# Weight-block sums of a gated-mixer decoder layer: added into SBUF during the MLP, or made in DRAM beforehand

## The chip, the core and the metric

The kernel is one program on one core of a Trainium2 chip. The metric is device time in microseconds of one execution, median of the runs shown. The core has five engines with a queue each: TensorE (PE; its weight loads are PEld), VectorE (DVE), ScalarE (ACT), GpSimd (POOL) and SyncE (SP), which here only issues transfers. All transfers, whoever issues them, run on the core's 16 DMA engines. Transfers that add to what stands at their destination are issued by POOL (queue q0); plain ones are issued by SP (q1) or ACT (q10).

## The reference

One layer, 512 tokens of width 1024, all float32:

```python
h = rms_norm(x, norm_mix_pre)
z = h @ w_in                                  # 10 parts of 1024 columns
y_a = a_b * causal_dwconv(a_c * a_h, conv_a_w)                   # 3 taps
y_c = silu(layer_norm(causal_dwconv(c_a * sigmoid(c_g), conf_dw_w) + conf_dw_b))   # 31 taps
y_s = spatial_gating(gelu(s_u), gelu(s_v), ...)                  # causal 128 x 128 per head
merged = sigmoid(g_a)*(y_a @ w_branch[0]) + sigmoid(g_c)*(y_c @ w_branch[1]) + sigmoid(g_s)*(y_s @ w_branch[2])
x = x + rms_norm(merged @ w_out, norm_mix_post)
f = square(relu(rms_norm(x, norm_ffn_pre) @ w_ff1)) @ w_ff2      # 1024 -> 4096 -> 1024
x = x + rms_norm(f, norm_ffn_post)
```

## The kernel before

**Units.** Weights are loaded and used in units of 512 KB, [128 partitions x 1024] float32, numbered 0 to 223. Each unit is split in two for precision: ACT copies it to `w_hi` (float32r, line 683), DVE subtracts to get `w_lo` (line 1066), and TensorE makes three products, hi*hi, lo*hi and hi*lo (lines 1590 to 1594, or 1775 to 1779 in the MLP's up product). `w_hi` and `w_lo` are rings of four units (`RING`), so ACT and DVE split unit u+4 when TensorE has done unit u. Up to the MLP the raw weights go through two slots (`RAW`): SP loads unit u (line 457) when DVE has split unit u-2.

**Stages**, by the profile's time: units 0 to 7, the spatial branch's `v` (to 52 us); the mixer, eight tiles of six units with the taps of both convolutions on DVE (52 to 322 us); the gates, 24 pairs of a gate unit and a branch unit (322 to 585 us), in whose first eight pairs DVE has the last nine taps of each convolution tile; the output projection (to 629 us); the MLP (629 to 953 us).

**Beside the gates**, POOL sums the convolution's channels tile by tile (`chan_sum`, lines 625 and 628), each when DVE has finished the tile's taps, and TensorE needs the sum behind the tenth pair (line 1736). In a pair ACT first makes a tanh of the gate (line 825), then splits unit u+4, then waits for the branch unit and splits unit u+5; DVE splits, does taps, gates the branch with the tanh (line 1249), splits, does taps.

**The MLP** runs in four quarters (`q`) of the hidden width, each an UP and a DOWN product. Both are 2 x 2 block products done in seven multiplications instead of eight: products 1, 2, 3 take one block of the weights, product 5 the sum of two blocks, 7 of two, 6 of three, 4 of four (by adding one more block to what product 5, then 6, left in its slot). A block is two units. The sums are made in SBUF: POOL issues transfers of a block's unit that add to a slot (`add_block`, line 646, 50 of 512 KB), and for product 7 SP loads a second block into slots 0 and 1 beside it (`side_load`) and DVE adds them (`sum_beside`, line 1389, 14 times). SP's order (`ff_load`, line 506) is written out by hand with waits behind sums. At the product changes TensorE waits until DVE has joined earlier products out of PSUM (line 1399).

**The start.** While TensorE does units 0 to 7, the row factors 1/rms are found; ACT copies them to `row_rstd` (line 758) behind the split of unit 6, and TensorE's unit 4 waits for it before its last block. DVE multiplies a table of taps by 0.5 (`cols`) right behind its first splits.

Of the kernel before, what the change touches and what calls it, by code (L numbers as in the profile page):

```python
# [25 lines left out]
F32 = mybir.dt.float32  # L26
F32R = mybir.dt.float32r
ALU = mybir.AluOpType
# [60 lines left out]
LOADED = {1: (0, 0), 2: (1, 0), 3: (1, 1), 5: (0, 0)}  # L89
ADDED = {5: (0, 1), 6: (1, 1), 4: (1, 0), 7: (0, 1)}  # L90
SLOTS = 10


def slot_of(f, product):
    return {1: 0, 2: 2, 3: 6, 7: 6}.get(product, 8 if f == DOWN else 4)
# [12 lines left out]
def stands_alone(u):  # L108

    return piece_of(u)[:3] == (QUARTERS - 1, DOWN, 7)  # L110


def is_loaded(u):
    return piece_of(u)[2] in LOADED or stands_alone(u)


def by_dma(u):
    return piece_of(u)[2] in (5, 6, 4) or stands_alone(u)


def ff_slot(u):
    _, f, product, h = piece_of(u)
    return (4 if stands_alone(u) else slot_of(f, product)) + h


def earlier_in_slot(u):
    return [v for v in range(U_FF, u) if ff_slot(v) == ff_slot(u)]


def ff_loads(u):  # L130
    many = sum(is_loaded(v) for v in earlier_in_slot(u))
    return 16 * (U_FF // RAW + 2 * many + 1 if ff_slot(u) < RAW else many + 1)


def side_loads(q, f):

    return 16 * (U_FF // RAW + 2 * (2 * q + f) + 2)


def sums_beside(q, f, h):  # L140

    return 2 * (2 * q + f) + h + 1


def sums_in_slot(u):
    return 16 * (sum(by_dma(v) for v in earlier_in_slot(u)) + 1)


def source(u, added=False):

    q, f, product, h = piece_of(u)
    k_half, n_half = (ADDED if added else LOADED)[3 if not added and stands_alone(u) else product]
    if f == DOWN:
        k_half = 1 - k_half
    at = 2 * (2 * k_half + n_half) if f == UP else CH * n_half + 2 * k_half
    return U_FF + (2 * q + f) * BLOCK_UNITS + at + h
# [81 lines left out]
def build(nc, x_d, xt_d, gain_d, units_d, cols_d, rows_d, ws_d, bs_d, out_d):  # L238
    kept_d = nc.dram_tensor("mixed_kept", (SEQ, D), F32, kind="Internal").ap()
    with ExitStack() as ctx:  # L240
# [108 lines left out]
        summed = sem("summed")  # L349
        raw_added = [sem(f"raw_added{n}") for n in range(SLOTS)]  # L350
# [104 lines left out]
        def _(sp):  # L455
# [29 lines left out]
            def ff_load(q, f, product, halves=(0, 1)):  # L485
                for h in halves:
                    u = ff_unit(q, f, product, h)
                    slot = ff_slot(u)
                    if earlier_in_slot(u) and slot < RAW:
                        sp.wait_ge(summed, sums_beside(q, f, h) - 2)  # L490
                    elif earlier_in_slot(u):
                        sp.wait_ge(w_lo_ready, earlier_in_slot(u)[-1] + 1)
                    elif slot < 2:
                        sp.wait_ge(w_lo_ready, u - RAW + 1)
                    elif slot < 4:
                        sp.wait_ge(spatial_done, KT)
                        sp.wait_ge(a_step, 3 * KT)
                        sp.wait_ge(s_step, 3 * KT)
                    elif slot < 6:
                        sp.wait_ge(y_c_lo, KT)  # L500
                    elif slot < 8:
                        sp.wait_ge(mixed_in, 4 * CH)
                    else:
                        sp.wait_ge(mixed_kept[CH - 2 + h], 16)
                        sp.wait_ge(sumsq_ready, 4 * CH)
                    sp.dma_start(slots[slot], units_d[source(u)]).then_inc(raw_loaded[slot], 16)
# [10 lines left out]
            for c in range(CH):  # L517
                if c == CH - 1:
                    ff_load(0, UP, 3)
# [1374 lines left out]
```

## Time and profile before

| | us |
|---|---|
| median of 3 runs | 960.39 |
| lowest, highest | 959.5, 963.52 |
| the profiled execution | 961.98 |
| its span, first to last instruction | 960.2 |
| TensorE busy | 949.0 |
| DVE, ACT, POOL busy | 730.8, 431.0, 104.5 |
| DMA moved | 142.84 MB |

The span is what the trace covers; the profiled execution took 1.8 us more around it. A busy time is what an engine's instructions cover, ends of matmuls modelled. A view of waits counts idle time of an engine ahead of an instruction and names what ended it; the chain that ended last is followed back from the last instruction, each step to what released it.

### The profile page before, as it was taken

Reading aid. Unit: us, or ns where it says so; the run is one execution under the profiler, and the core shown is the slowest. Engines: PE = TensorE matmul, PEld = TensorE weight load, DVE = VectorE, ACT = ScalarE, POOL = GpSimd, SP = SyncE. Lnnn points to the kernel's source line nnn. Section 1 sums busy time; section 2 is a strip of 40 time slices with the busy share of each in tenths; the row PEclk is TensorE's granted clock in tenths of the full one; section 3 lists DMA queues with packets and bytes.
Section 4 is the critical chain, followed back from the end, with each engine's and each line's share of the span. In section 5 each row is a group of like instructions: output and inputs, shape, how many; then the busy total and the mean of one; then the engine's idle time right before and its main releaser. Section 6 shows DMA issues by size and latency. Waiting matters only on the chain.

```text
span 960.2 us, 13424 instructions
## 1 busy us (share of the span) xinstructions
PE 949.0 (99%) x4838; PEld 808.8 (84%) x4838; DVE 730.8 (76%) x854; ACT 431.0 (45%) x534; POOL 104.5 (11%) x128
## 2 busy tenths in 40 slices
PE   9999999999999999999999999999999999999997
PEld 7788888888888888888888888899889889979985
DVE  4579888888888988886585344599975886796698
ACT  6543333333333322224374223467645745754674
POOL 1100001000100011113100000131101101111111
PEclk9999999999999999999999999999999999999999
DMA  8333333323223232224235333477989579778974
GB/s 313 106 113 105 110 93 93 110 93 93 93 93 103 66 103 94 88 88 131 88 101 207 113 106 112 173 203 198 255 267 244 158 211 244 169 180 256 257 189 131
DMA packets 40731, 142.84 MB, mean 149 GB/s; under 512 B 4720, under 2 KB 4848, under 8 KB 40688
## 3 DMA queue, kind: packets, MB, share of 16 engines
q1 hardware_dynamic: 31728, 111.32, 33.4%
q0 software_dynamic: 7712, 27.27, 15.5%
q10 hardware_dynamic: 1248, 3.67, 1.0%
q8 instruction: 27, 0.44, 0.2%
q14 instruction: 16, 0.13, 0.0%
HBM read 138.05 MB, written 4.19 MB: 148 GB/s over the span
## 4 chain that ended last, share of the span: by engine, by line
PE 82%; DMA 10%; DVE 4%; ACT 2%; issue 1%; SPq 0%; POOL 0%; ACTq 0%; DVEq 0%
PE ps L1590 25%; PE ps L1594 25%; PE ps L1592 25%; DMA glu<-units_in 6%; DMA raw_d<-units_in 2%; PE ps L1775 2%; DVE w_lo L1066 2%; PE ps L1777 2%; PE ps L1779 2%; ACT w_hi L683 1%; DMA raw<-units_in 1%; PE ps L1716 1%; DMA cols<-cols_in 1%; DMA glu<-xt_in 1%; ACT h L960 0%
## 5 line engine op out<-in xcount | busy, mean ns | idle before, releaser
L1590 PE MATMUL ps<-a_hi,w_hi 128*128 128x512 f32 x576 | 225.7, 392 | 0.0
L1592 PE MATMUL ps<-a_lo,w_hi 128*128 128x512 f32 x576 | 224.2, 389 | 0.0
L1594 PE MATMUL ps<-a_hi,w_lo 128*128 128x512 f32 x576 | 224.1, 389 | 0.0
L1066 DVE TENSOR_TENSOR w_lo<-raw,w_hi 128x1024 fp32r<-128x1024 f32 (+1 forms) x125 | 153.1, 1228 | 87.8 <-ACT w_hi L683 87.2
L683 ACT ACTIVATE w_hi<-raw 128x1024 fp32r<-128x1024 f32 (+1 forms) x125 | 130.2, 1048 | 184.7 <-PE ps L1594 103.7
L1149 DVE SCALAR_TENSOR_TENSOR conf<-glu,cols,conf (+1 forms) x240 | 186.8, 778 | 27.5 <-DVE conf L1149 26.4
L1590 PEld LDWEIGHTS ps<-a_hi,w_hi 128*128 128x128 f32 x576 | 108.1, 188 | 22.7 <-issue 0.5
L1592 PEld LDWEIGHTS ps<-a_lo,w_hi 128*128 128x128 f32 x576 | 108.2, 188 | 22.6 <-issue 0.5
L1594 PEld LDWEIGHTS ps<-a_hi,w_lo 128*128 128x128 f32 x576 | 108.2, 188 | 22.5
L1066 DVE TENSOR_TENSOR w_lo<-glu,w_hi 128x1024 fp32r<-128x1024 f32 x56 | 67.6, 1221 | 38.1 <-ACT w_hi L683 37.9
L1590 PE MATMUL ps<-w_hi,h_hi 128*128 128x512 f32 x224 | 88.0, 393 | 0.6 <-DVE wide L1424 0.2
L1594 PE MATMUL ps<-w_hi,h_lo 128*128 128x512 f32 x224 | 87.3, 390 | 0.0
L1592 PE MATMUL ps<-w_lo,h_hi 128*128 128x512 f32 x224 | 87.3, 390 | 0.0
L683 ACT ACTIVATE w_hi<-glu 128x1024 fp32r<-128x1024 f32 x56 | 58.1, 1053 | 51.5 <-DMA glu<-units_in 21.8
L1775 PE MATMUL ps<-x_plain_hi,w_hi 128*128 128x256 f32 x256 | 73.6, 288 | 1.3 <-DVE h L1399 0.7
L1777 PE MATMUL ps<-x_plain_lo,w_hi 128*128 128x256 f32 x256 | 72.4, 283 | 0.0
L1779 PE MATMUL ps<-x_plain_hi,w_lo 128*128 128x256 f32 x256 | 72.4, 283 | 0.0
L1775 PE MATMUL ps<-x_diff_hi,w_hi 128*128 128x256 f32 x192 | 54.5, 284 | 0.0
L1777 PE MATMUL ps<-x_diff_lo,w_hi 128*128 128x256 f32 x192 | 54.3, 283 | 0.0
L1779 PE MATMUL ps<-x_diff_hi,w_lo 128*128 128x256 f32 x192 | 54.3, 283 | 0.0
L1590 PEld LDWEIGHTS ps<-w_hi,h_hi 128*128 128x128 f32 x224 | 42.0, 188 | 12.3 <-DVE w_lo L1066 2.9
L1775 PEld LDWEIGHTS ps<-x_plain_hi,w_hi 128*128 128x128 f32 x256 | 49.0, 191 | 3.3 <-DVE h L1399 2.4
(177 smaller groups left out, 1608.1 us busy)
## 6 DMA issues: line engine op xcount, KB each, us to landing
raw<-units_in SPq DMA_DIRECT2D x141, 512.0 KB, 3.3
glu<-units_in SPq DMA_DIRECT2D x26, 512.0 KB, 6.7
glu<-units_in POOLq DMA_DIRECT2D x26, 512.0 KB, 8.2
raw_d<-units_in POOLq DMA_DIRECT2D x24, 512.0 KB, 6.8
raw_v<-units_in SPq DMA_DIRECT2D x16, 512.0 KB, 6.2
raw_d<-units_in SPq DMA_DIRECT2D x8, 512.0 KB, 6.5
conf<-x_in SPq DMA_DIRECT2D x4, 512.0 KB, 7.4
conf<-x_in ACTq DMA_DIRECT2D x1, 2048.0 KB, 7.8
```

What stands on the lines that cost most here:

```text
L683: return nc.scalar.activation(dst, src, ACT.Copy, scale=scale)
L1066: return nc.vector.tensor_tensor(dst, src, hi, ALU.subtract)
L1149: nc.vector.scalar_tensor_tensor(out=conf[:, tile, :], in0=glu[:, tile, k:k + SEQ], scalar=cols[:, tile, COL_CONF + k:COL_CONF + k + 1], i ...
L1590: nc.tensor.matmul(ps[:, bank, :], left_hi, right_hi, start=first, stop=False, skip_group_check=on_top)
L1592: nc.tensor.matmul(ps[:, bank, :], left_hi, right_lo, start=False, stop=False, skip_group_check=on_top)
L1594: return nc.tensor.matmul(ps[:, bank, :], left_lo, right_hi, start=False, stop=final, skip_group_check=on_top)
L1716: mm = nc.tensor.matmul(ps[:, 6, c * P:(c + 1) * P], v_tile[:, c, :], ws_raw[:, b, :], start=True, stop=True)
L1775: nc.tensor.matmul(out, w_hi[:, u % RING, w], hi[:, k, :], start=not free and k == 0, stop=False, skip_group_check=free)
L1777: nc.tensor.matmul(out, w_hi[:, u % RING, w], low[:, k, :], start=False, stop=False, skip_group_check=free)
L1779: mm = nc.tensor.matmul(out, w_lo[:, u % RING, w], hi[:, k, :], start=False, stop=k == CH - 1, skip_group_check=free)
```

## The change

The sums of weight blocks are no longer made in the MLP. A new DRAM tensor `weight_sums` holds, for each of the eight matrices (four quarters, UP and DOWN), four sums of 1 MB: for products 5, 7, 6 and 4.

- In the mixer ACT issues four copies of 1 MB per tile (`copy_first`), one per sum, of its first block from the weights to `weight_sums`: 32 in all. From the third tile on it first waits for the copies of the tile two earlier.
- POOL adds the other blocks with accumulating transfers of 1 MB, DRAM to DRAM, 8192 bytes a packet: for product 5 one per mixer tile, for products 7 and 6 two per channel sum in the gates, for product 4 eight in a row behind the sums of squares. 32 in all.
- In the MLP SP loads all 112 units plainly, in order, into ten slots in turn. `add_block`, `side_load`, `sum_beside` and the waits behind sums are gone.
- Two edits elsewhere: ACT copies `row_rstd` ahead of the split of unit 6 instead of behind it, and DVE scales the taps behind units 0 to 7 instead of ahead.

```diff
+PLAIN = {1: (0, 0), 2: (1, 0), 3: (1, 1)}
+SUMS = (5, 7, 6, 4)
+FIRST_BLOCK = {5: (0, 0), 7: (1, 1), 6: (1, 1), 4: (1, 0)}
+SECOND_BLOCK = {5: (0, 1), 7: (0, 1)}
 def ff_slot(u):
-    _, f, product, h = piece_of(u)
-    return (4 if stands_alone(u) else slot_of(f, product)) + h
+    return (u - U_FF) % SLOTS
...
+    sums_d = nc.dram_tensor("weight_sums", (MATRICES * BLOCK_UNITS, P, D), F32, kind="Internal").ap()
...
+            def ff_load(u):
+                q, f, product, h = piece_of(u)
+                slot = ff_slot(u)
+                if u - U_FF >= SLOTS:
+                    sp.wait_ge(w_lo_ready, u - SLOTS + 1)
...
+                if product in PLAIN:
+                    src = units_d[U_FF + (2 * q + f) * BLOCK_UNITS + block_at(f, PLAIN[product]) + h]
+                else:
+                    src = sums_d[(2 * q + f) * BLOCK_UNITS + sum_at(product) + h]
+                sp.dma_start(slots[slot], src).then_inc(raw_loaded[slot], 16)
+            for n in range(4):
+                ff_load(U_FF + n)
+            for f in range(2):
+                sp.wait_ge(two_summed[f], 16 * QUARTERS)
+                sp.wait_ge(side_summed[f], 16 * QUARTERS)
+                sp.wait_ge(three_summed[f], 16 * QUARTERS)
+                sp.wait_ge(four_summed[f], 16 * QUARTERS)
...
+            def two_blocks(m, product, summed):
+                q, f = divmod(m, 2)
+                copies = len(SUMS) * (q + 1 if product == 5 else QUARTERS)
+                pool.wait_ge(first_copied[f], 16 * copies)
+                at = U_FF + m * BLOCK_UNITS + block_at(f, SECOND_BLOCK[product])
+                pool.dma_start(sum_of(m, product), units_d[at:at + 2].rearrange("h p n -> (h p) n"),
+                               accum_op=ALU.add, max_dma_last_dim=SUM_BYTES).then_inc(summed[f], 16)
+            def three_blocks(m):
+                pool.wait_ge(two_summed[f], 16 * QUARTERS)
+                pool.dma_start(sum_of(m, 6), sum_of(m, 5), accum_op=ALU.add, ...)
+            def four_blocks(m):
+                pool.wait_ge(three_summed[f], 16 * QUARTERS)
+                pool.dma_start(sum_of(m, 4), sum_of(m, 6), accum_op=ALU.add, ...)
             for j in range(KT):
...
                 mask_spatial(j % 2, 32 * (j // 2 + 1))
+                if j:
+                    two_blocks(j - 1, 5, two_summed)
+            two_blocks(MATRICES - 1, 5, two_summed)
             for j in range(KT):
+                two_blocks(j, 7, side_summed)
+                three_blocks(j)
                 pool.wait_ge(conf_tap, KT * (N_OWN + N_NEXT) + N_LATE * (j + 1))
...
+            for m in range(MATRICES):
+                four_blocks(m)
...
+            def copy_first(j, f, product):
+                source = j.times(BLOCK_UNITS, U_FF + block_at(f, FIRST_BLOCK[product]))
+                into = j.times(BLOCK_UNITS, sum_at(product))
+                act.dma_start(sums_d[bass.ds(into, 2)].rearrange("h p n -> (h p) n"),
+                              units_d[bass.ds(source, 2)].rearrange("h p n -> (h p) n")
+                              ).then_inc(first_copied[f], 16)
             def mix_tile(u, j, b):
+                if j.first >= 2:
+                    act.wait_ge(first_copied[b], Count(j.first // 2, j.i, 1).times(16 * len(SUMS)))
+                copy_first(j, b, 5)
                 after(u)
...
                 split_hi(u.plus(RING))
+                copy_first(j, b, 7)
...
                 split_hi(u.plus(3 + RING))
+                copy_first(j, b, 6)
...
                 split_hi(u.plus(4 + RING))
+                copy_first(j, b, 4)
...
-                split_hi(u.plus(RING))
                 if n == CH - 2:
                     act.wait_ge(rstd_spread, 1)
                     nc.scalar.activation(row_rstd[:, :], ps[:, 2 * CH - 1, :], ACT.Copy).then_inc(row_rstd_ready, 1)
+                split_hi(u.plus(RING))
```

On ACT, in the body of the mixer's loop, from the tanh of the conformer's gate (`duo`) to the copy into `y_a`. Before:

```order
L774 ACTIVATE duo<-ps 128x512
L687 ISA
L683 ACTIVATE w_hi<-raw 128x1024
L708 REGISTER_ALU
L683 ACTIVATE w_hi<-raw 128x1024
L779 REGISTER_ALU
```

and with the change:

```order
L722 DMA weight_sums<-units_in 16x16384
L658 ISA
L734 ISA
L735 ACTIVATE duo<-ps 128x512
L643 ISA
L639 ACTIVATE w_hi<-raw 128x1024
L722 ISA
L722 DMA weight_sums<-units_in 16x16384
L658 REGISTER_ALU
L639 ACTIVATE w_hi<-raw 128x1024
L741 REGISTER_ALU
```

The copy for product 5 now stands ahead of the wait for TensorE's first unit of the tile, the one for product 7 behind that unit's split. Each is 16 rows of 16384 float32, 64 KB a row.

On POOL, from the last mask of the spatial weights (`ws_raw`) over the channel sums (`u_act`). Before:

```order
L594 DMA ws_raw<-ws_in 128x128 [waits s_step]
L595 DMA bs_row<-bs_in 128x128
L601 AFFINE_SELECT ws_raw<-ws_raw 128x128 [waits spatial_loaded1]
L625 COPY u_act<-conf 128x512 [waits s_step,conf_tap]
L628 TENSOR_TENSOR u_act<-u_act,conf 128x512 [waits chan_sum,conf_tap] x7
```

and with the change:

```order
L552 AFFINE_SELECT ws_raw<-ws_raw 128x128 [waits spatial_loaded1]
L575 DMA weight_sums<-units_in 128x2048 [waits first_copied0]
L575 DMA weight_sums<-units_in 128x2048 [waits first_copied1]
L575 DMA weight_sums<-units_in 128x2048 [waits first_copied0]
L582 DMA weight_sums<-weight_sums 128x2048 [waits two_summed0]
L608 COPY u_act<-conf 128x512 [waits s_step,conf_tap]
L575 DMA weight_sums<-units_in 128x2048 [waits first_copied1]
L582 DMA weight_sums<-weight_sums 128x2048 [waits two_summed1]
L611 TENSOR_TENSOR u_act<-u_act,conf 128x512 [waits chan_sum,conf_tap]
```

Two accumulating transfers with their waits now stand ahead of each channel sum; the eight sums stood in a row.

On SP, from the second of the raw slots' last loads into the MLP's loads. Before:

```order
L511 DMA raw<-units_in 128x1024 [waits w_lo_ready] x2
L506 DMA raw_d<-units_in 128x1024 [waits sumsq_ready,mixed_kept2,raw_added5]
L506 DMA raw_d<-units_in 128x1024 [waits sumsq_ready,mixed_kept3]
L506 DMA raw<-units_in 128x1024 [waits summed,raw_added9]
L506 DMA raw<-units_in 128x1024 [waits summed]
```

and with the change:

```order
L481 DMA raw_d<-weight_sums 128x1024 [waits sumsq_ready,mixed_kept2]
L481 DMA raw_d<-weight_sums 128x1024 [waits sumsq_ready,mixed_kept3]
L481 DMA raw<-weight_sums 128x1024 [waits w_lo_ready] x2
L481 DMA raw_v<-weight_sums 128x1024 [waits w_lo_ready] x2
L481 DMA glu<-weight_sums 128x1024 [waits w_lo_ready] x2
```

The loads of second blocks (line 511) and the waits for sums are gone; a load waits only for DVE's split of the unit that had the slot.

## Rows read from the trace of the kernel before

**Rows 1.** The page: the span, and section 1, each engine's busy time
```profile
span 960.2 us, 13424 instructions
...
PE 949.0 (99%) x4838; PEld 808.8 (84%) x4838; DVE 730.8 (76%) x854; ACT 431.0 (45%) x534; POOL 104.5 (11%) x128
```

**Rows 2.** Busy time by stage: busy us (x instructions) by engine, PEclk, DMA, GB/s
```profile
52.00:322.00 270.00, 270.00 (x1232) 224.94 (x1231) 227.34 (x301) 90.88 (x116) 15.73 (x22) 1.00 0.31 99
...
336.00:431.00 95.00, 95.00 (x421) 78.69 (x420) 84.86 (x99) 21.94 (x25) 16.98 (x8) 1.00 0.28 93
...
629.00:953.00 324.00, 322.12 (x2037) 290.02 (x2035) 263.28 (x268) 197.80 (x223) 46.44 (x56) 1.00 0.81 214
953.00:960.00 7.00, 0.19 (x1) 0.00 (x0) 4.70 (x8) 1.02 (x3) 0.00 (x0) 0.68 0.40 150
```

**Rows 3.** Waits of the weight loads, whole run: us in total, times, longest
```profile
PEld ps L1590 <- DVE w_lo L1066: 2.9, 8, 0.5
PEld ps L1775 <- DVE h L1399: 2.4, 7, 0.9
...
PEld ps L1590 <- ACT y_s L758: 1.3, 1, 1.3
```

**Rows 4.** POOL in order of time, gates: start, us, instruction [idle before <- releaser]
```profile
368.48 2.21 POOL L628 TENSOR_TENSOR u_act<-u_act,conf 128x512 f32<-128x512 f32 x1 [9.55 <-DVE conf L1149]
...
427.27 2.21 POOL L628 TENSOR_TENSOR u_act<-u_act,conf 128x512 f32<-128x512 f32 x1 [9.55 <-DVE conf L1149]
```

**Rows 5.** TensorE in order of time, where the first half of the gates ends
```profile
431.14 1.02 PE L1736 MATMUL ps<-u_act,mean_of 128*128 128x512 f32 x2
```

**Rows 6.** Chain that ended last, 10 to 40 us: start, us, what
```profile
19.12 5.59 DMA cols<-cols_in
...
27.47 6.77 DMA raw<-units_in
34.29 0.50 PE ps L1590
```

**Rows 7.** Groups by line, MLP: xcount | busy, mean ns | idle
```profile
L1389 DVE TENSOR_TENSOR glu<-glu,raw 128x1024 f32<-128x1024 f32 x14 | 16.7, 1216 | 0.0
```

**Rows 8.** Chain that ended last, first quarter of the MLP
```profile
712.26 7.19 DMA raw_d<-units_in
...
720.27 8.80 DMA glu<-units_in
...
731.78 10.67 DMA glu<-units_in
```

**Rows 9.** SP's loads for the MLP (line 506): starts, time to landing
```profile
L506 SPq DMA_DIRECT2D glu<-units_in x26: 327/430/737, 603.6 to 907.7; - x26
...
DMA to landing us min/median/max: 3.1/6.0/13.7
```

**Rows 10.** Transfers at 669:671 and 658:665 us, by queue at 677:683
```profile
DMA packets 210, 0.79 MB, mean 397 GB/s; under 512 B 16, under 2 KB 16, under 8 KB 210
...
DMA packets 398, 1.43 MB, mean 205 GB/s; under 512 B 48, under 2 KB 48, under 8 KB 398
...
q0 software_dynamic: 222, 0.84, 70.3%
q1 hardware_dynamic: 222, 0.79, 35.4%
```

**Rows 11.** SP's weight loads in the gates (line 457), 322 to 431 us
```profile
DMA to landing us min/median/max: 3.1/3.2/3.4
```

**Rows 12.** All engines in order of time, one pair of the gates
```profile
375.93 5.86 SPq L457 DMA_DIRECT2D raw<-units_in  x2
...
379.24 1.06 ACT L683 ACTIVATE w_hi<-raw 128x1024 fp32r<-128x1024 f32 x1 [5.19 <-DMA raw<-units_in]
...
382.46 0.60 ACT L825 ACTIVATE duo<-ps 128x512 f32<-128x512 f32 x1 [2.16 <-PE ps L1594]
...
385.71 0.68 DVE L1249 SCALAR_TENSOR_TENSOR wide<-duo,ps 128x512 f32 x1
```

More of the change, by code:

```diff
@@ L105, in piece_of, with block_at, sum_at @@
     return q, f, ORDER[f][n // 2], n % 2
[L108 to L118, printed above, removed]
 def ff_slot(u):
-    _, f, product, h = piece_of(u)
-    return (4 if stands_alone(u) else slot_of(f, product)) + h
-def earlier_in_slot(u):
-    return [v for v in range(U_FF, u) if ff_slot(v) == ff_slot(u)]
+    return (u - U_FF) % SLOTS
 def ff_loads(u):
[L131 to L156, printed above, removed]
+    many = (u - U_FF) // SLOTS + 1
+    return 16 * (U_FF // RAW + many if ff_slot(u) < RAW else many)
+def block_at(f, block):
+    k_half, n_half = block
+    return 2 * (2 * k_half + n_half) if f == UP else CH * n_half + 2 * (1 - k_half)
+def sum_at(product):
+    return 2 * SUMS.index(product)
 def up_bank(q, product):
@@ L484, in _ @@
                     load(i * RAW + slot, slot)
[L485 to L506, printed above, removed]
@@ L517, in _ @@
+            for n in range(4):
[5 more added lines that the diff above has]
+                sp.wait_ge(four_summed[f], 16 * QUARTERS)
+            for n in range(4, 6):
+                ff_load(U_FF + n)
             for c in range(CH):
                 if c == CH - 1:
-                    ff_load(0, UP, 3)
+                    for n in range(6, 8):
+                        ff_load(U_FF + n)
@@ L549, in _ @@
+            for u in range(U_FF + 8, UNITS):
+                ff_load(u)
             sp.wait_ge(unit_done, ff_unit(QUARTERS - 1, UP, 4, 1) + 1)
@@ L695, in ff_hi @@
                 slot = ff_slot(u)
[L696 to L702 removed]
+                act.wait_ge(raw_loaded[slot], ff_loads(u))
                 if free:
@@ L1469, in _ @@
                     split_behind(q, UP, 2, 1)
-                    for h in range(2):
-                        sum_beside(q, UP, h)
                 done(q, UP, 5, 0)
@@ L1475, in _ @@
                     x_lo("21-22-11", 10)
-                    for h in range(2):
-                        sum_beside(q, UP, h)
                 done(q, UP, 5, 1)
@@ L1539, in _ @@
                         add_product(q, product, 0)
-                    if product == 3 and q < QUARTERS - 1:
-                        sum_beside(q, DOWN, 1)
                     last_set = {1: "21+12-11-22", 2: "21-22-11", 3: "11-21"}.get(product)
@@ L1544, in _ @@
                         set_lo(q, last_set)
-                    if product == 2 and q < QUARTERS - 1:
-                        sum_beside(q, DOWN, 0)
                     if q == QUARTERS - 1 and product == 6:
```

116 lines of the change are left out of this document (33 added, 83 removed).

## The prediction

> **What bounds the kernel now.** I read the page's engine lines first, then the busy time by stage, then what TensorE's weight loads waited for, and last the queues of the transfers. TensorE is busy 949.0 of 960.2 us [rows 1]. Of the 11.2 us left, 6.8 us lie behind 953 us, where the last sums are weighed and stored, and 1.9 us in the whole MLP (629 to 953 us) [rows 2]; the other 2.5 us lie at the start. Its granted clock is full (1.00 of 2.4 GHz) in every stage up to 953 us, and the matmuls stay the same in number and size. So a gain can come only from those waits. The waits at its weight loads are 1.3 us for the row factor near 34 us, and in the MLP 2.9 us on DVE's weight splits and 2.4 us on DVE's joins [rows 3]; about 6.6 us in all is the most that can come back. The profiled execution took 961.98 us, its span is 960.2 us, the median of three is 960.39 us: I make the sum on 961.98 and take 1.6 us off.
>
> What could cost time is everything under that full TensorE. The first half of the gates (322 to 431 us) is the weak place: from 336 us on DVE is busy 84.9 of 95 us [rows 2] and is slower than TensorE. One pair of gate and branch takes DVE 11.75 us (POOL's channel sums follow it, and from 368.48 to 427.27 us they stand 58.8/5 us apart [rows 4]) and TensorE 48 matmuls of 0.227 us, 10.9 us. At the end POOL's last channel sum ends at 427.27 + 2.21 = 429.5 us [rows 4], and the matmul that reads it starts at 431.14 [rows 5]: 1.7 us are left. Each us by which DVE falls further back than that is a us of the kernel.
>
> **The start.** ACT copies the row factor (y_s) behind the split of unit 6, which waits for a load that is late, since DVE sat in the column scaling until the columns landed (5.59 us in the chain, then a load of 6.77 us, and at 34.29 us TensorE goes on [rows 6]). Its weight load had waited 1.3 us [rows 3]. The change scales the columns behind the loop and copies the factor ahead of the split, so both reasons go. What is late next is the factor itself, which then waits only for four small matmuls inside unit 3, one unit ahead of the first that needs it. **-1.2 us.** The 0.3 us scaling moves into DVE's time before the statistics; its reader on ACT is the first mixer tile, later than both.
>
> **The MLP.** Gone: 50 accumulating transfers of 512 KB, 14 side loads, 14 additions on DVE of 1.216 us, 17 us [rows 7]. What is left are 112 plain loads into ten slots: a slot comes round every ten units of 324/112 = 2.9 us [rows 2], against 6.0 us median and 13.7 us longest from issue to landing [rows 9]. The waits on joins trace back to accumulates: the chain before 745 us is a load of 7.19 us, then two accumulates of 8.80 and 10.67 us, then ACT, DVE, and the join [rows 8]. Those waits go. (Five us of waits show as only 1.9 us of idle matmuls, since a weight load is fetched ahead of its matmul and ends of matmuls are modelled.) Part of the waits on splits stays: at a change of product TensorE needs two units at once, and ACT and DVE must have split both. Of 5.3 us I take half: **-2.5 us** (0 to -5.3).
>
> **The mixer (52 to 322 us).** New on ACT: 32 copies of 1 MB, DRAM to DRAM, in 16 pieces of 64 KB. Their issue costs some 0.45 us each on ACT, which is busy 90.9 of 270 us [rows 2]: hidden. The copies share the 16 DMA engines with the weight loads. At full load the engines moved plain packets at 397 GB/s and accumulating ones at 205 GB/s [rows 10]: 1.3 us for a load of 512 KB, 5.1 us for an accumulate of 1 MB. No row shows a transfer from DRAM to DRAM. Lower bound for a copy of 1 MB: one pass, 2.6 us. Upper: read and write each count, 5.3 us. A tile of 33.8 us (270/8) then has six loads (7.9), four copies (10.6 to 21) and one accumulate (5.1 to 7.9): 24 to 37 us. I take the lower end, because the accumulate into SBUF shows that a write beside two reads costs no third pass (205 is 397 halved). A load that meets a piece of 64 KB lands after 3.2 us [rows 11] and 2.6 more; its slot has two units, 10.9 us, less 2.3 us for both splits and 0.4 us of issue: 8.2 us. **0 us.** If that cover is gone, the ring of four units still holds about 12 us.
>
> **The gates.** New on POOL: in each of eight pairs two accumulates of 1 MB ahead of the channel sum, which stands behind only their issue (0.9 us each as now in the MLP, inside the 9.5 us in which POOL idles before each sum [rows 4]). The channel sums are now queued on POOL behind waits for the copies of the last mixer tile; these land by about 322 us, long before the sums that bind [rows 4]. The load beside an accumulate is what costs. From 677 to 683 us both queues had work, and both moved 222 packets in 6.0 us [rows 10]: they alternate packet by packet, 0.48 us for one of each on one engine. The new accumulates have packets of 8 KB, 0.32 us more: 0.80 us. A load is eight packets on each engine, so it takes 3.2 - 1.3 + 8 x 0.80 = 8.3 us against 3.2 us now [rows 11]. The deadline: the load issued at 375.93 us is split by ACT at 379.24; behind it stands the tanh (0.60 us) that DVE's gating at 385.71 us reads [rows 12]. 385.71 - 0.60 - 1.06 - 0.1 - 375.93 = 8.0 us. So each pair is late by 0.3 us, 2.1 us over the seven pairs beside which accumulates run. And the engines are over-full: 2 x 5.1 + 2 x 1.3 = 12.9 us of work per 11.75 us, which bounds the delay at 8 us. I take 3.5 us, near the lower end, since alternation gives the loads their turn before the accumulates. Less the 1.7 us left: **+1.8 us** (0 to +6.3).
>
> **Behind the gates.** The eight last accumulates, 41 us, are issued behind POOL's sums of squares, in the second half of the gates. SP waits for them before the load at 603.6 us [rows 9]; from 464 us (an estimate: three pairs behind 431) they have 139 us for 41, or 63 at three passes: hidden. Where they run, a pair of loads needs 8.3 + 2.7 = 11.0 us a slot against TensorE's 10.9: hidden by the ring.
>
> **Sum.** 961.98 - 1.2 - 2.5 + 1.8 = 960.1, less 1.6: **958.5 us**, no change within 0.5% (955.6 to 965.2 us), which is about what a measurement of this kernel can tell from none.
>
> **Rivals.**
> *DRAM counts every pass (slower).* If source, destination and write each take DMA time, a packet of 8 KB takes 3 x 0.32 = 0.96 us and a load in the gates 1.9 + 8 x (0.96 + 0.16) = 10.9 us, 2.9 us past the deadline: 20 us over seven pairs. The engines then have 15.4 + 2.6 = 18.0 us of work per 11.75 us, at most 44 us. Between them 33 us, less 1.7, and the last eight accumulates (63 us) hold each pair of units for 13.6 instead of 10.9 us, 12 us of which the ring hides half: +37 us in place of +1.8, **994 us**. It decides from 0.66 us per packet on, where the delay passes 5 us; between there and 0.96 lie 965 to 994 us. For it: no row shows a transfer that writes to DRAM beside reads from DRAM. Against it: the accumulate's rate, in which a write beside two reads is free. The destination is another memory there, so I give it **0.30**.
> The Trainium skill, "DMA: Bandwidth & Descriptors", Latency and other measured facts, gives 207 to 214 GB/s per direction for copies between HBM tensors, half of the 397 GB/s seen here for loads; an estimate by that page is 5 us for a copy of 1 MB, the upper end above. No run so far can show whether it holds here; by it this rival's 994 us would be the forecast.
> *The copies fill the mixer (slower).* Pieces of 64 KB at two passes hold an engine 5.3 us, and a load that meets two waits 10.6 us more, 13.9 us, beyond 8.2 us twice a tile; ACT's stalls then delay DVE, which is busy 227 of 270 us and has little to catch up with [rows 2]. From the second tile whose lag is not recovered it costs about 1.5 us a tile: +12 us, **970 us**. **0.12**.
> *All waits go (faster).* 961.98 - 6.6 - 1.6 = **953.8 us**, with the gates free because accumulates are quicker than 0.62 us a packet. **0.12**.
> *The MLP's waits stay* because DVE's own queue makes them (it is busy 263 of 324 us [rows 2]): 961 us, within the forecast's band; it is part of its **0.46**.
>
> **How the numbers follow.** Faster 0.12, within 0.5% 0.46, slower 0.42. The forecast's own range is 955.6 to 965.2. The range that holds 8 in 10 leaves out below 954.5 (0.08) and above 992 (0.12).
>
> **What would show it.** Start: TensorE without a wait at 34 us. Gates: time from issue to landing of the weight loads, 3.2 us now; 8.3 if I am right, about 11 by the first rival; the channel sums' spacing, 11.75 us now, 12.2 or 14 to 17; TensorE's idle time before the first mean matmul. Mixer: loads under 8 us and DVE's waits on ACT. MLP: no wait of POOL or ACT on an accumulate, joins no longer in the chain. I am wrong if a packet of 8 KB takes other than 0.62 to 0.66 us, if the queues do not alternate one to one with pieces of 64 KB, or if the MLP's waits have another cause.

## The result and the profile after

The changed kernel takes 978.06 us (median of four runs, 975.95 to 981.55), the kernel before beside it 961.22 us: a ratio of 1.018, 95% interval 1.016 to 1.020. It is slower by 1.8%, 16.8 us. The forecast of 958.5 us was wrong: the gain that it named came and was larger than forecast, and about 21 us in the trace (23 us by the medians, e4 below) came on top, nearly all of it in two places that it had priced at 1.8 and at 0 us. The profiled execution took 975.95 us, the shortest of the four. Its page: the span, engines, and the queues of the transfers (q1 SP's loads, q0 POOL's accumulating transfers, q10 ACT's copies: packets, MB, share of 16 engines):

```profile
span 974.2 us, 13524 instructions
...
PE 950.8 (98%) x4838; PEld 812.1 (83%) x4838; DVE 712.9 (73%) x840; ACT 429.9 (44%) x534; POOL 78.3 (8%) x110
...
q1 hardware_dynamic: 36336, 128.10, 37.4%
q0 software_dynamic: 5120, 34.61, 18.5%
q10 hardware_dynamic: 2272, 37.23, 9.9%
```

TensorE has the same 4838 instructions and 1.8 us more of busy time than in [rows 1], so 12 of the 14 us of span are waits. The busy time by stage (columns as in [rows 2]) says in which stage:

```profile
52.00:322.00 270.00, 270.00 (x1232) 224.97 (x1231) 222.55 (x295) 90.41 (x115) 17.85 (x29) 1.00 0.77 248
336.00:431.00 95.00, 88.97 (x381) 71.71 (x380) 74.44 (x92) 19.87 (x23) 21.22 (x21) 0.98 0.96 231
...
431.00:590.00 159.00, 150.34 (x647) 123.15 (x646) 88.21 (x102) 62.66 (x85) 19.05 (x16) 0.97 0.62 177
...
629.00:953.00 324.00, 323.97 (x2077) 296.01 (x2077) 251.08 (x252) 202.34 (x231) 9.14 (x17) 1.00 0.55 188
```

The mixer is untouched (270.00 of 270, with 248 GB/s in place of 99). The stretch from 629 to 953 us has next to no idle time left, where [rows 2] had 322.12 of 324; the MLP itself now begins some 20 us later. The gates lose 6.0 us before 431 us, with the transfer engines at a share of 0.96, and 8.7 us behind it. And the waits of the weight loads (us in total, times, longest):

```profile
PEld ps L1539 <- DVE b_lo L1031: 9.1, 1, 9.1
PEld ps L1539 <- DVE w_lo L1030: 8.6, 7, 3.3
```

Against [rows 3]: the waits on joins (h) and on the row factor (y_s) are gone; the waits on splits (w_lo) have moved from the MLP to the gates; and one wait of 9.1 us is new, on the last part of the layer norm's result (b_lo).

**The first half of the gates.** The weight loads' times from issue to landing, first 322 to 431 us, then 464 to 526 us:

```profile
DMA to landing us min/median/max: 3.3/10.3/11.5
...
DMA to landing us min/median/max: 3.2/10.7/12.0
```

Before, the median was 3.2 us in the first stretch [rows 11] and 3.3 us in the second (longest 7.1). POOL's channel sums, one a pair of units:

```profile
384.38 1.30 POOL L611 TENSOR_TENSOR u_act<-u_act,conf 128x512 f32<-128x512 f32 x1 [9.84 <-DVE conf L1113]
...
422.52 1.28 POOL L611 TENSOR_TENSOR u_act<-u_act,conf 128x512 f32<-128x512 f32 x1 [9.61 <-DVE conf L1113]
436.57 1.29 POOL L611 TENSOR_TENSOR u_act<-u_act,conf 128x512 f32<-128x512 f32 x1 [11.19 <-DVE conf L1113]
```

From 384.38 to 422.52 us are three pairs of 12.7 us, where [rows 4] had 11.76. Two slots for raw weights carry one pair: a slot is free again after 10.3 us for the load, 1.06 us for ACT's split, 1.23 us for DVE's and 0.1 us between, and that is 12.7 us. A second limit lies at the same place. SP's queue carries both loads of a pair, and from 385 to 400 us the accumulates (q0) and the loads (q1) moved:

```profile
q0 software_dynamic: 349, 2.56, 82.2%
q1 hardware_dynamic: 332, 1.23, 21.6%
```

At 1.23 MB in 15 us, two loads of 0.524 MB take 12.8 us. Their packets follow one another almost without a gap (384.01 to 390.24, 390.81 to 396.51, 397.04 to 402.75 us), so by this limit more slots alone would not shorten the pair. No run here tells the two limits apart. The last sum comes 9.3 us later than the last of [rows 4].

**The layer norm.** The chain that ended last, ahead of the matmul that waited:

```profile
512.27 3.46 issue
515.74 1.06 ACT w_hi L639
516.79 0.71 ACT glu L820
...
522.29 0.69 DVE glu L1259
522.98 0.61 DVE b_lo L1031
523.60 0.04 issue
523.64 0.80 PE ps L1539
```

Read it backwards. TensorE needs b_lo; b_lo needs four tiles of ACT's affine and tanh steps (L820, L824), one every 1.37 us from 516.79 to 522.27; and these stand on ACT behind a weight split (w_hi) that began only at 515.74 us. The profile calls the time ahead of it "issue", but the load that it needed was issued at 505.50 us and landed at 515.66 us. The profile shows no wait of TensorE on the weights here; what was late is the work queued behind their split.

**The clock.** Both stalls are followed by a stretch at a lower granted clock (the number behind the engines, as in [rows 2]); between the two windows stands the matmul that ended the first stall:

```profile
408.00:432.00 24.00, 19.58 (x78) 15.38 (x77) 16.92 (x22) 5.21 (x6) 5.73 (x6) 0.93 1.02 242
...
426.96 0.51 PE L1539 MATMUL ps<-a_hi,w_hi 128*128 128x512 f32 x1 [2.87 <-DVE w_lo L1030]
...
504.00:528.00 24.00, 15.34 (x59) 12.23 (x58) 16.43 (x23) 16.43 (x27) 0.00 (x0) 0.82 0.77 198
```

Inside them matmuls start 0.43 us apart in place of 0.227, from 426.96 to 430.3 us and from 523.6 to 529.5 us: 1.2 in place of 2.4 GHz, worth about 1.7 and 2.9 us.

**Where the 14 us of span come from.** Both traces have 4838 matmuls, so the start of the n-th in one can be set against the start of the n-th in the other. By this measure the changed kernel is 0.8 us ahead at 52 us and still at the end of the mixer, loses 9.2 us in the first half of the gates (to 440 us), loses 11.6 us at the layer norm (500 to 530 us), and gains 6.3 us in the MLP: 13.7 of 14.0 us. The median of the four executions is another 2.1 us above the traced one; no trace shows where those lie.

### The profile page after: what moved, and what is told of

Its sections match the earlier page's. It is cut to its first block, busy times and chain, and to the rows that moved or that the text cites. A ratio compares the mean times of both kernels' runs of the same rounds, so it can differ in the third digit from the quotient of the medians.

```text
span 974.2 us, 13524 instructions
## 1 busy us (share of the span) xinstructions
PE 950.8 (98%) x4838; PEld 812.1 (83%) x4838; DVE 712.9 (73%) x840; ACT 429.9 (44%) x534; POOL 78.3 (8%) x110
## 3 DMA queue, kind: packets, MB, share of 16 engines
q10 hardware_dynamic: 2272, 37.23, 9.9%
## 4 chain that ended last, share of the span: by engine, by line
PE 65%; DVE 15%; DMA 11%; issue 5%; ACT 2%; DVEq 2%; SPq 0%; ACTq 0%
PE ps L1539 16%; PE ps L1541 16%; PE ps L1543 16%; DMA raw<-units_in 11%; DVE conf L1113 7%; PE ps L1724 6%; PE ps L1726 6%; PE ps L1728 6%; DVE w_lo L1030 4%; ACT w_hi L639 1%; DVEq L1113 1%; DVE y_a L1164 1%; PE ps L1619 1%; DVE y_s L1185 0%; DMA gain<-gain_in 0%
## 5 line engine op out<-in xcount | busy, mean ns | idle before, releaser
L1030 DVE TENSOR_TENSOR w_lo<-raw,w_hi 128x1024 fp32r<-128x1024 f32 (+1 forms) x133 | 164.1, 1237 | 118.6 <-ACT w_hi L639 118.4
L639 ACT ACTIVATE w_hi<-raw 128x1024 fp32r<-128x1024 f32 (+1 forms) x133 | 138.6, 1049 | 214.6 <-DMA raw<-units_in 144.3
L1113 DVE SCALAR_TENSOR_TENSOR conf<-glu,cols,conf (+1 forms) x240 | 181.4, 756 | 27.5 <-DVE conf L1113 26.4
L1030 DVE TENSOR_TENSOR w_lo<-glu,w_hi 128x1024 fp32r<-128x1024 f32 x44 | 52.7, 1221 | 18.9 <-ACT w_hi L639 18.9
L639 ACT ACTIVATE w_hi<-glu 128x1024 fp32r<-128x1024 f32 x44 | 45.0, 1050 | 36.4 <-PE ps L1543 28.6
L1539 PE MATMUL ps<-b_hi,w_hi 128*128 128x512 f32 x128 | 51.1, 400 | 9.2 <-DVE b_lo L1031 8.7
L1541 PE MATMUL ps<-b_lo,w_hi 128*128 128x512 f32 x128 | 50.8, 397 | 0.0
```

The source lines that it names most:

```text
L639: return nc.scalar.activation(dst, src, ACT.Copy, scale=scale)
L1030: return nc.vector.tensor_tensor(dst, src, hi, ALU.subtract)
L1113: nc.vector.scalar_tensor_tensor(out=conf[:, tile, :], in0=glu[:, tile, k:k + SEQ], scalar=cols[:, tile, COL_CONF + k:COL_CONF + k + 1], i ...
L1539: nc.tensor.matmul(ps[:, bank, :], left_hi, right_hi, start=first, stop=False, skip_group_check=on_top)
L1541: nc.tensor.matmul(ps[:, bank, :], left_hi, right_lo, start=False, stop=False, skip_group_check=on_top)
```

## The experiments

Ratios are to the kernel before, run beside. All edits are to the changed kernel, but for e3 (to the kernel before), e9 (to e5), e10 and e11 (to e8) and e12 (to e10).

**e4: the accumulating transfers left out.**

```
             for j in range(KT):
-                two_blocks(j, 7, side_summed)
-                three_blocks(j)
...
-            for m in range(MATRICES):
-                four_blocks(m)
```
(and the eight calls for product 5; SP waits for the copies.)

> The change without its 32 accumulating transfers: the copies and the MLP's plain loads stay; the additions of weight blocks are left out, so the result is not the layer's. Theory: all the loss comes from the accumulates' traffic beside the gates, and the copies cost nothing: before less 1 us at the start less about 6 us of waits in the MLP, 954 to 955 us. Rival: the copies or their issue on ACT also delay the gates: 957 us or more.

The 32 additions are left out. Measured: 955.1 us, ratio 0.9935 (0.9916 to 0.9954). The first line is the stretch from 900 us of the kernel before, the second the same of e4:

```profile
900.00:953.00 53.00, 52.88 (x287) 45.35 (x285) 47.52 (x57) 34.79 (x46) 7.33 (x10) 1.00 0.68 180
```
```profile
900.00:953.00 53.00, 45.99 (x234) 39.07 (x232) 47.69 (x59) 31.26 (x45) 2.87 (x4) 0.96 0.39 138
```

TensorE has 6.9 us less left at 900 us. So the plain MLP, with the edits of the start, is worth 6.2 us of time, the copies cost nothing by themselves, and the 32 accumulating transfers cost all the rest, 978.06 - 955.1 = 23 us.

**e1: packets of 4 KB in place of 8 KB.**

```
-SUM_BYTES = 8192
+SUM_BYTES = 4096
```

> The change with packets of 4 KB in place of 8 KB in all 32 accumulating transfers; the bytes are the same. Theory (turns): the two queues alternate packet by packet, so a weight load of eight packets an engine costs 8 x (0.16 + packet time of the accumulate); at 0.63 us that is 6.3 us of engine time, two loads a pair 12.6 us, more than the 11.75 us of a pair. At 0.33 us it is 3.9 us, 7.8 us a pair: loads land after about 6 us instead of 10.3, both stalls of TensorE (about 410 and 515 us) go, and the time is 955 to 958 us. Rival (capacity): what binds is the engines' total work, 2 x 5.0 + 2 x 1.3 = 12.6 us per pair of 11.75 us; it is slightly larger with 4 KB packets (0.656 for 0.628 us), so the stalls stay and the time is 978 to 980 us.

Measured: 968.51 us, ratio 1.0078 (1.0049 to 1.0107), between the two theories. The same bytes in the same place cost 9.5 us less, so the amount alone is not the cause. Loads of the gates (322 to 431 us), and below the seam of mixer and gates:

```profile
DMA to landing us min/median/max: 3.3/8.0/8.6
...
322.00:336.00 14.00, 11.14 (x43) 8.74 (x42) 12.47 (x17) 4.25 (x6) 2.67 (x3) 0.88 0.71 184
```

The slot's cycle is 8.0 + 2.4 = 10.4 us, under 11.76, and the channel sums are 11.76 us apart again. But loads land in 8.0 us, not the 6 that I had expected. One load shows why: SP issues it, and here is what q0 and q1 moved from 371.5 to 374.5 us and then from 374.7 to 378.7 us.

```profile
371.31 0.33 SPq L430 DMA_DIRECT2D raw<-units_in  x1
...
q0 software_dynamic: 153, 0.61, 102.5%
q1 hardware_dynamic: 15, 0.04, 3.8%
...
q0 software_dynamic: 151, 0.57, 71.7%
q1 hardware_dynamic: 139, 0.52, 34.8%
```

The 15 packets of q1 in the first stretch are the end of the load before, until 372.4 us; then the accumulates have the engines to themselves. The new load's 128 packets of data begin at 374.8 us, 3.5 us after the issue, and then the queues do alternate (151 to 139). In the kernel before a load's first packet comes 1.0 us after its issue. The seam's 3 us of idle time (4.7 us by the starts, with the lower clock) are new and are the next question.

**e2: the last eight accumulates after the layer norm.**

```
+            pool.wait_ge(y_c_lo, KT)
             for m in range(MATRICES):
                 four_blocks(m)
```

> The change with the eight last accumulates (product 4) issued only when the layer norm's result is split (y_c_lo, about 523 us), instead of behind the sums of squares (468 us). Theory: the second stall (8.8 us at 514.6 us and the clock that falls with it, 2.9 us) is made by these eight: ACT waits for late weight loads, and the norm's steps stand behind those splits. Without them beside the norm the stall goes, the first one stays: 978 - 11.7 = 966 to 967 us. Rival: the second stall is only the delay of the first half of the gates handed on through the channel sums; then it stays at 6 to 9 us and the time is 974 to 978 us.

Measured: 972.55 us, ratio 1.0126 (1.0104 to 1.0148).

```profile
PEld ps L1540 <- DVE w_lo L1031: 15.4, 11, 3.0
...
PEld ps L1540 <- DVE b_lo L1032: 0.3, 1, 0.3
```

The norm's wait is gone (9.1 to 0.3 us), so it did come from the transfers beside it. By the starts 4.5 us of it return as waits on splits in the second half of the gates, where loads beside packets of 8 KB again miss the pair's period. Another 3.4 us are lost in the first half, which this edit does not touch: in this trace DVE comes out of the mixer 3.9 us later than in that of the changed kernel. A time between the two expectations: right on the place, wrong that the place is free.

**e3: the two edits of the start alone, on the kernel before.**

```
-                split_hi(u.plus(RING))
                 if n == CH - 2:
                     act.wait_ge(rstd_spread, 1)
                     nc.scalar.activation(row_rstd[:, :], ps[:, 2 * CH - 1, :], ACT.Copy).then_inc(row_rstd_ready, 1)
+                split_hi(u.plus(RING))
...
-            dve.wait_ge(cols_loaded, 16)
-            taps = cols[:, :, COL_CONF:COL_CONF + CONF_K]
-            nc.vector.tensor_scalar(taps, taps, 0.5, None, ALU.mult).then_inc(cols_scaled, 1)
...
+            dve.wait_ge(cols_loaded, 16)
+            taps = cols[:, :, COL_CONF:COL_CONF + CONF_K]
+            nc.vector.tensor_scalar(taps, taps, 0.5, None, ALU.mult).then_inc(cols_scaled, 1)
             statistics(1)
```

> The kernel before with only the two small edits of the change: the row factor copied ahead of unit 6's split, and the taps scaled behind the first units. Theory: TensorE's gap of 1.24 us at 33 us goes, -0.9 to -1.2 us (960.0 to 960.3 of 961.2). Rival: the time is given back before the mixer starts, 0 us.

Measured: 961.07 us against 961.3, ratio 0.9999 (0.9986 to 1.0013). The gap is closed:

```profile
34.00:52.00 18.00, 18.00 (x81) 14.89 (x80) 14.96 (x23) 11.62 (x16) 0.00 (x0) 1.00 0.27 87
```

but by the starts of the matmuls it gives 0.6 us, and the runs do not resolve it.

**e5 to e8: copies in small pieces, packets of 2 and 4 KB, early and late.** All four have this edit:

```
-                              units_d[bass.ds(source, 2)].rearrange("h p n -> (h p) n")
-                              ).then_inc(first_copied[f], 16)
+                              units_d[bass.ds(source, 2)].rearrange("h p n -> (h p) n"),
+                              max_dma_last_dim=4096).then_inc(first_copied[f], 16)
```

> The kernel after with accumulating transfers in packets of 4 KB (as e1_pkt4k, 968.5 us) and, new, ScalarE's sixteen copies in pieces of 4 KB in place of 64 KB. Theory: pieces of 64 KB (2.5 us each) that alternate with a load's packets made single loads of the mixer land 12 to 15 us late, ScalarE's and VectorE's steps stood behind the split of such a load, that lag (8.0 us at the end of the mixer in e1, against the kernel without accumulates) was carried to the seam of mixer and gates and cost 3.0 us there and some 1.7 us at the lower clock: no mixer load over 10 us, lag under 2 us, the seam without a stall, 962 to 965 us. Rival: the lag comes from the accumulates of the mixer or from the amount of bytes, not from the pieces' size: 967 to 970 us, lag 6 us or more.

> As e5, with accumulating packets of 2 KB. Theory (turns: a load packet waits for one packet of the other queue): a load of 8 packets an engine needs 8 x (0.16 + about 0.17) = 2.6 us of turns, gates' loads land in 5 to 6.5 us (8.0 in e1), the stall at the norm's steps (5.8 us in e1 and some 1 to 2 at the lower clock) shrinks to under 2 us: 956 to 960 us. Rival (what counts is the total of bytes in the stretch, or small accumulating packets cost more than a quarter of an 8 KB one): at or over e5's time, 963 to 970 us.

> As e6, and the last eight accumulates (four blocks) are issued only after the layer norm's result is split (as in e2, whose norm had no stall but 15.4 us of weight waits). Theory: neither the norm nor the second half of the gates stalls, the MLP's gain of some 6 us stays: 954.5 to 957.5 us, under the kernel before by 0.4 to 0.7%. Rival: the eight accumulates collide with the loads of the second half even at 2 KB, or land after the MLP's load asks for them: 960 us or more, with waits on w_lo at 530 to 600 us.

> As e7 with accumulating packets of 4 KB: tells the packet size from the place of the accumulates. Theory of turns: loads land in about 8 us as in e1, which the weight ring just bears outside the norm: 956 to 960 us, 1 to 3 us over e7. If place alone counts: the same as e7. If the size alone counts: as e5.

| | accumulates | copies | last eight | us | ratio, 95% interval |
|---|---|---|---|---|---|
| after | 8 KB | 64 KB | early | 978.06 | 1.0181 (1.0161, 1.0200) |
| e1 | 4 KB | 64 KB | early | 968.51 | 1.0078 (1.0049, 1.0107) |
| e5 | 4 KB | 4 KB | early | 963.29 | 1.0030 (1.0016, 1.0044) |
| e6 | 2 KB | 4 KB | early | 960.17 | 0.9991 (0.9974, 1.0008) |
| e7 | 2 KB | 4 KB | late | 958.88 | 0.9983 (0.9969, 0.9998) |
| e8 | 4 KB | 4 KB | late | 956.29 | 0.9949 (0.9936, 0.9963) |

e5 came out nearly as expected (there are 32 copies, not sixteen): its mixer loads and its seam are

```profile
DMA to landing us min/median/max: 3.0/4.4/10.3
...
322.00:336.00 14.00, 14.00 (x63) 11.62 (x62) 12.79 (x18) 3.04 (x5) 2.67 (x3) 1.00 0.93 214
```

The longest mixer load is 10.3 us, 14.0 in e1 and 15.4 in the changed kernel. Set beside e4, DVE splits the same unit 2.2 us later at the seam, in e1 8.0 us later: in the mixer DVE is busy 218 to 227 of 270 us and hands most of a lag on, unit after unit, until the seam, where TensorE needs DVE's result at once. Kernels with the same mixer show how far this lag varies. With accumulating packets of 4 KB it is 8.0 and 7.8 us with the large pieces (e1, e11) and 2.2, 1.8 and 0.8 us with the small ones (e5, e8, e9), a clear difference. With packets of 8 KB it is 2.4 and 6.3 us with the large pieces (the changed kernel, e2) and 6.1 and 4.0 us with the small ones (e10, e12), none that these traces resolve.

The norm's wait is still there:

```profile
PEld ps L1539 <- DVE b_lo L1031: 5.1, 1, 5.1
```

e8 has neither; here the page's span, then 336 to 431 and 490 to 530 us:

```profile
span 953.5 us, 13525 instructions
...
336.00:431.00 95.00, 94.92 (x420) 78.14 (x418) 84.77 (x99) 20.03 (x23) 28.91 (x22) 1.00 0.99 237
...
490.00:530.00 40.00, 40.00 (x178) 32.90 (x177) 22.98 (x33) 20.44 (x31) 7.18 (x8) 1.00 0.67 199
```

Its span is that of e4 (953.2 us) with all sums made. This version beats both kernels, the one before by 0.5%. I had expected it 1 to 3 us over e7; it is 2.6 us under it. e6 (960.17 us) just missed its range, with 2.7 us left of the norm's wait, and e7 missed its own. Its loads in the gates do land earlier, as turns say:

```profile
DMA to landing us min/median/max: 3.1/6.7/8.7
```

but its mixer loads take 5.2 us in the median (4.5 in e8) and DVE comes to the seam 5.0 us later than in e4 (1.8 in e8); from 400 to 480 us TensorE then loses some 4 us more than before, by the starts of its matmuls, at places where POOL's or DVE's steps are due. That smaller accumulating packets get fewer bytes a turn, last longer and so meet more loads of the mixer fits this; no run isolates it.

**e9: the norm's steps ahead of the split.**

```
-                behind_branch(u)
                 for t in SILU_TILES.get(j, ()):
...
                     copy_hi(b_hi[:, t, :], nrm[:, t, :], 0.5).then_inc(y_c_hi, 1)
+                behind_branch(u)
```
(and DVE's second `split_lo` in the same way.)

> The kernel of e5 (963.3 us; its largest wait is 5.1 us of TensorE on b_lo at the end of the layer norm). One edit: in the eight steps of the norm ScalarE and VectorE do the affine, tanh and silu steps of a unit's tiles ahead of that unit's second weight split, in place of behind it. All transfers and their order stay. Theory (the norm's steps are late because they stand behind a split that waits for a late load): the wait on b_lo falls under 1 us, and if the splits keep their slack, 957 to 960 us; what the weight ring can't bear shows as waits on w_lo at 480 to 530 us. Rival (VectorE and ScalarE have simply too much work there, or the clock fell first): b_lo waits 4 us or more wherever the split stands, 962 to 965 us.

Measured: 961.61 us, ratio 1.0003 (0.9991 to 1.0015), against 963.29 for e5.

```profile
PEld ps L1539 <- DVE b_lo L1031: 2.4, 1, 2.4
...
490.00:530.00 40.00, 38.04 (x168) 31.15 (x168) 24.47 (x34) 22.10 (x32) 0.00 (x0) 1.00 0.95 278
```

The order on ACT and DVE is part of that wait (5.1 to 2.4 us here), with no transfer moved and no new waits on splits. By the median the edit gives 1.7 us, with no overlap of the intervals of e5 and e9 (1.0016 to 1.0044 against 0.9991 to 1.0015). This trace is the fastest of its twelve runs (957.31 us, 4.3 us under their median), so the wait is read at its best, and the share is an upper one. An earlier split, of the same pair, still stands ahead of the steps; that it makes the rest was not tested.

**e10: e8 with packets of 8 KB.**

```
-SUM_BYTES = 4096
+SUM_BYTES = 8192
```

> The kernel of e8 (956.3 us) with accumulating packets of 8 KB again: tells whether packets of 4 KB are needed once the copies are in small pieces and the last eight accumulates are late. Theory (turns: a pair of loads needs 2 x 8 x (0.16 + 0.63) = 12.6 us in a period of 11.75 us): the waits on w_lo between 380 and 430 us are back as in after (some 6 us of waits and 2 to 3 at the lower clock), the channel sums come 12.5 us or more apart: 964 to 969 us. Rival (the mixer's late loads and the norm's place made the whole loss): 956 to 959 us.

Measured: 973.09 us, ratio 1.0106 (1.0077 to 1.0135). The waits on splits are back:

```profile
PEld ps L1540 <- DVE w_lo L1031: 16.2, 14, 2.9
...
336.00:431.00 95.00, 88.57 (x383) 71.22 (x383) 76.98 (x94) 18.25 (x21) 22.10 (x21) 1.00 0.98 236
...
530.00:629.00 99.00, 94.61 (x412) 76.42 (x411) 39.00 (x43) 28.72 (x39) 1.26 (x4) 1.00 0.74 215
```

I had expected 964 to 969, since I had counted only the first half of the gates; between 530 and 629 us another 4.4 us go. At the seam, too, 1.5 us are lost, in spite of the small copies. The packet's size is the largest single factor, 16.8 us from e8 to e10, and with 8 KB the small copies give nothing (972.55 in e2).

**e11: e8 with copies in pieces of 64 KB.** The edit of e5 undone.

> The kernel of e8 (956.3 us) with ScalarE's copies in pieces of 64 KB again; accumulating packets stay at 4 KB and the last eight accumulates stay late. Tells what the copies' pieces are worth by themselves. If they make single mixer loads late and that lag costs at the seam of mixer and gates (as from e1 to e5, 5.2 us): 959 to 963 us, with the longest mixer load over 11 us and some loss between 322 and 336 us. Rival (e5's gain over e1 was only a smaller chance of a lag that the accumulates make): 956 to 958 us.

Measured: 959.6 us, ratio 0.9983 (0.9967 to 0.9998), 3.3 us over e8. Mixer loads and the seam:

```profile
DMA to landing us min/median/max: 3.0/4.6/14.8
...
322.00:336.00 14.00, 11.54 (x45) 9.10 (x44) 12.46 (x18) 3.21 (x6) 2.67 (x3) 0.88 0.74 185
```

In line with the first theory. Its runs lie between 955.7 and 962.98 us, and the trace is the slowest of them. That a load of the mixer meets two large pieces in some runs and not in others would explain this spread; it was not tested. In the trace of the changed kernel the lag at the seam was only 2.4 us, and the seam full.

**e12: one accumulate a pair beside the channel sums in place of two.** An edit to e10: packets of 8 KB, small copies, and now sixteen accumulates behind the norm.

```
             for j in range(KT):
                 two_blocks(j, 7, side_summed)
-                three_blocks(j)
...
+            for m in range(MATRICES):
+                three_blocks(m)
```

> The kernel of e10 (973.1 us: packets of 8 KB, copies in 4 KB, last eight accumulates late) with eight more accumulates (three blocks) taken from beside the channel sums and issued ahead of the last eight, after the norm: one transfer of 1 MB in each period of 11.75 us beside the channel sums in place of two. Theory (the queue of loads loses throughput, 12.6 us a pair, while an accumulate runs; one transfer fills only some 10 us of a period): a pair needs less than the period again, channel sums 11.8 us apart, no waits on w_lo from 336 to 431 us (PE 94.5 us or more of 95, 88.6 in e10). The sixteen late transfers then run past 603 us, so the second half of the gates waits more, and the MLP's loads behind the sums too: as a whole 965 us or more, which is not what is asked. Rival (each load is late whenever any accumulate is near, rate or not): PE under 92 us in that stretch.

Measured: 978.28 us, ratio 1.0175 (1.0150 to 1.0199). From 336 to 431 us, with its loads, and from 530 us:

```profile
336.00:431.00 95.00, 94.65 (x418) 78.09 (x417) 84.83 (x100) 20.99 (x24) 20.59 (x15) 1.00 0.69 169
...
DMA to landing us min/median/max: 3.1/3.4/6.1
...
530.00:629.00 99.00, 84.13 (x343) 65.10 (x341) 33.28 (x38) 25.93 (x32) 6.59 (x8) 0.95 0.98 247
```

With packets of 8 KB, but half as many accumulates, the stretch is clean, and the channel sums are 11.8 us apart. The eight that were moved cost more where they went: by the starts 22 us between 530 and 629 us.

## Why the prediction was wrong, point by point

**The start (-1.2 us).** The wait went as foretold, the gain did not: 0.8 us in the trace of the changed kernel, 0.6 in that of e3 and none in e3's runs.

**The MLP (-2.5 us, 0 to -5.3).** Right in kind, too small: -6.3 us by the starts, and -6.2 us in the median of e4, which has the start too. I had taken half of the 5.3 us of waits, since part of those on splits was to stay; e4 has none of them left. The waits were not the whole either, though the busy time by stage showed only 1.9 us idle. By the starts of the matmuls the kernel before had lost 6.7 us there, and e4 0.5: many small delays that busy times with modelled ends cover. "Part of the waits on splits stays" was the step that failed.

**The mixer (0 us).** Right for this kernel (270.00 of 270) and for copies alone (e4). Not seen was that single loads land only after 14 to 15 us where accumulates and pieces of 64 KB are both in the queues, and that DVE carries such a lag to the seam: with accumulating packets of 4 KB 3.3 us in e11 against e8, 5.2 in e1 against e5.

**The first half of the gates (+1.8 us, 0 to +6.3).** Right was that packets of 8 KB alternate with a load's one to one. From 391 to 393 us:

```profile
q0 software_dynamic: 45, 0.37, 88.3%
q1 hardware_dynamic: 41, 0.17, 22.2%
```

A packet of 8 KB takes 0.883 x 2 x 16 / 45 = 0.63 us, which I had assumed. Two steps failed. One is the term "3.2 - 1.3" of the load, taken as fixed: beside accumulates a load's first packet comes 3.5 us after its issue in the median and not 1.0, whatever their size. With 0.5 us for the end, 3.5 + 8 x (0.16 + p) + 0.5 gives 10.3, 7.9 and 6.7 us for packets of 0.63, 0.33 and 0.18 us; measured 10.3, 8.0, 6.7 (after, e1, e6; the parts came out as 3.6, 5.8 and 0.8 us for packets of 8 KB, so the middle one is a little less than the formula has). The other is the step from a load to a pair, "each pair is late by 0.3 us", which sets one load against ACT's deadline of 8.0 us. What binds is the pair: its slot's cycle, 12.7 us, and the turns of its two loads, which by the prediction's own 0.80 us are 2 x 8 x 0.80 = 12.8 us in a period of 11.75. The prediction had about that figure ("the engines are over-full") and used it only as an upper bound, on the ground that alternation gives the loads their turn first; but a turn for a load is a turn for an accumulate too. So each pair is late by 0.9 us and more, it adds up, and the clock falls behind it: +9.2 us.

**Behind the gates (0 us).** The failed step is "hidden by the ring". The ring of four units does hide a late weight from TensorE; it does not hide it from the layer norm's steps, which stand on ACT behind a split that waits for that load: 8.7 us of wait at the matmul and 2.9 us of clock, 11.6 us (removed by e2, and shortened by e9's order where it stood at 5.1 us). This and the term before it are the surprise: 960.1 of the sum, 11.6 and 9.2 - 1.8 more, 0.4 more for the start and 3.8 less for the MLP is 975.7 us, beside the 975.95 of the profiled execution.

**The rivals.** "DRAM counts every pass" is refuted by the 0.63 us, where it had 0.96. The time lies in the stretch that it opened (965 to 994 us) for another reason. The page named beside it, the Trainium skill's "DMA: Bandwidth & Descriptors", Latency and other measured facts, gives 207 GB/s for copies between HBM tensors whose rows lie 512 KiB apart, and 214 GB/s with a pitch of 4 MiB padded by 4 KiB. Here ACT's queue moved 37.23 MB in 9.9% of 16 x 974.2 us of engine time, 24 GB/s an engine or 386 GB/s for sixteen, close to the 397 of plain loads [rows 10]. So the copies here, whole contiguous blocks, do not follow these figures. "The copies fill the mixer" was right that pieces of 64 KB make single loads late and wrong about the price: no matmul of the mixer starts later, in any of the traces. "All waits go" gave 953.8 us; e4 is that case, 955.1.

**The range** of 954.5 to 992 us held the time; it did so by way of a rival that is refuted. What a range for the right reason needed was the question of what stands behind each wait on ACT.

## To carry to other kernels

When transfers are moved to where the engines are "idle", price them by what they do to the latency of the loads beside them: start delay, plus packets an engine times one packet of each queue, plus the splits, against the time in which the slots come round; and set the turns of all loads of a period against that period. Then read down the in-order queue of every engine that waits for such a load, and price what stands behind the wait, not only the loaded data. Keep the packets of background transfers no larger than those of the loads they share engines with (4 KB here; 2 KB was 3.1 us better with the last eight early and 2.6 us worse with them late, 8 KB cost 17 us), and leave out the stretches in which an engine's chain is bare.

## What the runs showed of the hardware

In the median a load's first packet came 1.0 us after its issue on free engines and 3.4 to 3.6 us after it beside accumulating transfers of another queue, alike for packets of 2, 4 and 8 KB. Accumulating packets took 0.178, 0.328 and 0.63 us for 2, 4 and 8 KB, the same DRAM to DRAM as before into SBUF, at 4 KB twice a plain one (0.159 us). A copy DRAM to DRAM took per 4 KB what a load took. After a stall of 2.9 us that followed others, and after one of 8.7 us, TensorE ran at 1.2 GHz for 3.4 and 6.1 us; after one of 2.4 us in e9 the granted clock of 490 to 530 us stayed 1.00. POOL's channel sum took 2.2 us beside DVE's tap steps (e12 and [rows 4]) and 1.3 us in the changed kernel, where DVE stood still at that moment (422.44 to 425.68 us); this was seen, not tested.
